# The residual transposed before it is normalized, the router put between output products, and the second block's loads asked for at other places

## What is computed

```python
def rms_norm(x, w):
    y = xf * lax.rsqrt(jnp.mean(xf * xf, axis=-1, keepdims=True) + NORM_EPS)
    return (y * w.astype(jnp.float32)).astype(x.dtype)

# layer 0 (block A)
h = h + ssd_memory_mixer(h, mem, a_norm_w[i], ...)     # ends in [y, m] @ out_w
h = h + hierarchical_moe(h, ffn_norm_w[0], ...)
# layer 1 (block B)
k_sh, v_sh = shared_kv(h, kv_norm_w, w_kv, positions)  # rms_norm(h) @ w_kv
h = h + swa_memory_mixer(h, k_sh, v_sh, mem, ...)      # rms_norm(h) @ in_w gives q and q_mem
h = h + hierarchical_moe(h, ffn_norm_w[1], ...)
return rms_norm(h, final_norm_w)

def hierarchical_moe(h, norm_w, rg_w, rg_b, re_w, re_b, w_gate, w_up, w_down):
    xt = rms_norm(h, norm_w).reshape(-1, d)
    group_p = jax.nn.softmax((xt @ rg_w) + rg_b)        # 4 groups, the best one
    exp_logits = (xt @ re_w) + re_b                     # 8 experts in a group, the best two
    ...
    for e in range(32):
        out = out + gates[:, e:e + 1] * ((silu(xt @ w_gate[e]) * (xt @ w_up[e])) @ w_down[e])
```

## Time and profile before

| | |
|---|---|
| three runs | 1459.13, 1455.79, 1454.13 us; median 1455.79 |
| the profiled execution, its own time | 1459.73 us |
| its span, first to last instruction | 1457.9 us (1.8 us less than its time) |
| PE, DVE, ACT, POOL busy | 1230.5, 278.1, 199.1, 33.4 us |
| read from HBM | 456.66 MB |
| mean granted TensorE clock | 0.919 of 2.4 GHz |

### The profile page before, as it was taken

One profiled execution on the slowest core, in us unless ns is written; L12 is line 12 of the kernel. 1 busy time (PEld: TensorE's weight loads), 2 busy tenths in 40 slices (PEclk: granted clock), 3 DMA queues, 4 the chain that ended last, 5 costly groups with the idle time before them and its releaser, 6 DMA issues. The chain is left out here.

```text
span 1457.9 us, 15099 instructions
## 1 busy us (share of the span) xinstructions
PE 1230.5 (84%) x6038; PEld 623.7 (43%) x6038; DVE 278.1 (19%) x691; ACT 199.1 (14%) x491; POOL 33.4 (2%) x42
## 2 busy tenths in 40 slices
PE   6999999889999997687643998979999999666664
PEld 6875874444443453232211466454444444222211
DVE  3542451221010100000002156022011101000001
ACT  3133231100000000000001145110000000000001
POOL 0001210000000000000000011000000000000000
PEclk9999999889999999889886999969999999778877
DMA  9534207459999999999998222538999999999994
GB/s 368 208 116 140 92 26 320 173 229 417 419 416 416 413 419 369 419 410 418 419 397 302 107 83 86 203 116 336 418 416 416 418 417 417 418 415 421 414 418 163
DMA packets 93897, 458.76 MB, mean 315 GB/s; under 512 B 7040, under 2 KB 7040, under 8 KB 60672
## 3 DMA queue, kind: packets, MB, share of 16 engines
q1 hardware_dynamic: 93824, 457.74, 78.3%
HBM read 456.66 MB, written 1.05 MB: 314 GB/s over the span
## 5 line engine op out<-in xcount | busy, mean ns | idle before, releaser
L1358 PE MATMUL bank<-own,e_xg 128*64 128x512 f32 (+1 forms) x1312 | 279.6, 664 | 41.4 <-DMA own<-in_w_up 18.4
L1358 PE MATMUL bank<-late,e_xg 128*64 128x512 f32 (+1 forms) x736 | 181.9, 676 | 35.6 <-DMA own<-in_w_up 19.5
L1367 PE MATMUL bank<-own,e_turned 128*32 128x512 f32 (+1 forms) x656 | 146.8, 707 | 48.2 <-DMA own<-in_w_down 34.3
L1358 PEld LDWEIGHTS bank<-own,e_xg 128*64 128x64 f32 (+1 forms) x1312 | 80.8, 134 | 199.1 <-issue 199.0
L1250 DVE TENSOR_TENSOR e_hid<-e_silu,bank 128x512 f32<-128x512 f32 x24 | 16.5, 688 | 515.0 <-ACT e_silu L1301 515.0
L1367 PE MATMUL bank<-late,e_turned 128*64 128x512 f32 (+1 forms) x368 | 91.0, 699 | 21.9 <-DMA own<-in_w_down 9.1
L1358 PEld LDWEIGHTS bank<-late,e_xg 128*64 128x64 f32 (+1 forms) x736 | 51.2, 135 | 133.8 <-issue 133.8
L1333 PE MATMUL bank<-e_pick,xs 128*128 128x128 f32 x768 | 101.1, 287 | 3.9 <-DVE e_pick L1197 2.3
L1333 PEld LDWEIGHTS bank<-e_pick,xs 128*128 128x128 f32 x768 | 94.1, 200 | 22.7 <-issue 18.0
L1367 PEld LDWEIGHTS bank<-own,e_turned 128*32 128x32 f32 (+1 forms) x656 | 41.2, 139 | 126.2 <-issue 119.5
L1301 ACT ACTIVATE e_silu<-bank 128x512 f32<-128x512 f32 x24 | 14.3, 597 | 554.9 <-PE bank L1358 554.9
(11 more groups left out here) (297 smaller groups left out, 1022.6 us busy)
## 6 DMA issues: line engine op xcount, KB each, us to landing
own<-in_w_up SPq DMA_DIRECT2D x83, 1024.0 KB, 14.3
own<-in_w_down SPq DMA_DIRECT2D x82, 1024.0 KB, 15.0
own<-in_w_gate SPq DMA_DIRECT2D x81, 1024.0 KB, 15.2
late<-in_w_gate SPq DMA_DIRECT2D x47, 1024.0 KB, 16.7
late<-in_w_down SPq DMA_DIRECT2D x46, 1024.0 KB, 14.2
late<-in_w_up SPq DMA_DIRECT2D x45, 1024.0 KB, 14.4
own<-in_a_in_w SPq DMA_DIRECT2D x18, 1024.0 KB, 12.1
own<-in_mem_w_kv SPq DMA_DIRECT2D x8, 1024.0 KB, 11.2
```

What stands on the lines that cost most here:

```text
L1358: ins = pe.matmul(bank[q * T:(q + 1) * T, :], self.xg[:, at:at + T], cut(tile(q), k=4)[:, k, :], start=(half == 0 and k == 0), stop=(half ...
L1367: ins = pe.matmul(self.b_down[out][q * T:(q + 1) * T, :], self.turned[:, at:at + T], cut(tile(q), j=2)[:, j, 512 * out:512 * out + 512], s ...
```

## The change

- **Residual transposed raw.** `x2T` (both routers) and `xT` (block B) transpose `h` itself. The factor is computed alongside: the logits are multiplied by it (`scalar_tensor_tensor` with the bias), in block B the evictions of q, k, v, and the softmax scale of the memory scores. The columns of the weights are laid out for that (`by_block`, `blocks`, `(k p)` in place of `(p k)`). The scaled `xs`, which the experts' gather reads, is now written by ACT.
- **Order of the end of a mixer.** The last tile's products are split by quarter, the transposes of t = 0 come after `("out", 1)`, its logits between `("out", 2)` and `("out", 3)`. Evictions of `x2T` alternate between ACT and DVE. `choose` works on all 32 experts at once and takes the group's mask afterwards; two chains are interleaved; the counts are separate products after the places.
- **Gather.** The second half goes to a bank of its own (`b_turn`).
- **Loads of block B.** Four (two tiles) are issued in `moe(c, 0)` ahead of the wait for the last down product; the other ten in `mixer_b`. q comes first, then kv; the first banks used are 4 to 7.
- **Final norm.** Its weight is loaded at the start of `moe(c, 1)` into an unused tensor.

```diff
-    NORMED = [("x2T", 0), ("x2T", 1), ("router", 0)]
-    UNITS = NORMED + [("x2T", 2), ("x2T", 3), ("router", 1), ("places", 0)]
+    UNITS = [("out", 0), ("out", 1), ("x2T", 0), ("x2T", 1), ("out", 2), ("router", 0), ("out", 3), ("x2T", 2), ("x2T", 3),
+             ("router", 1), ("places", 0)]
@@ out_rows
+    if i == 0:
+        for m in range(n, last):
+            some(0, m, (0, 1))
+    if i == 2:
+        for m in range(n + 1, last):
+            some(1, m, (0, 1)).then_inc(s["out_tile"], 1)
+    some(t, last, (i % 2,)).then_inc(c.units_done, 1)
+    if i == 1:
+        some(1, n, (0, 1)).then_inc(s["out_tile"], 1)
@@ Router.act
+        if kind == "x2T" and i % 2 == 0:
+            t = i // 2
             U.wait_done(act, key)
+            act.activation(self.x2T(i), cut(U.bank(key), k=4), ACT.Copy).then_inc(s["x2T_act"], 1)
+            act.wait_ge(s["h_new"], 2 * t + 2)
+            h, xs = cut(c.h, t=NT)[:, t, :], cut(c.xs[:, :], t=NT)[:, t, :]
+            act.activation(xs, h, ACT.Square, accum_out=self.ss[t]).then_inc(s["n2_act"], 1)
+            act.wait_ge(s["n2_dve"], 2 * t + 1)
+            act.activation(self.r[t], self.ss[t], ACT.Sqrt).then_inc(s["n2_act"], 1)
+            act.wait_ge(s["n2_dve"], 2 * t + 2)
+            act.activation(xs.rearrange("q (k p) -> q p k", k=KD), h.rearrange("q (p k) -> q p k", k=KD), ACT.Copy,
+                           scale=self.r[t]).then_inc(s["n2_act"], 1)
@@ Router.pe
-            pe.wait_ge(s["n2_dve"], 3 * t + 3)
+            pe.wait_ge(s["h_new"], i + 1)
+            transposes(c, pe, out, [cut(c.h, t=NT)[:, t, (4 * half + k) * P:(4 * half + k + 1) * P] for k in range(4)])
@@ Router.dve
+            dve.wait_ge(s["n2_dve"], 2 * i + 2)
+            dve.scalar_tensor_tensor(out=cut(self.lg, t=NT)[:, i, :], in0=U.bank(key)[:, 0:NG + NE], scalar=self.r[i],
+                                     in1=c.f(f"route_b{self.layer}"), op0=ALU.mult, op1=ALU.add).then_inc(s["rt_dve"], 1)
@@ Experts.block, sync
+                if layer == 1:
+                    final_w = c.ins["final_norm_w"].rearrange("(o n) -> o n", o=1)
+                    sp.dma_start(c.memT1[:, 0:D], final_w.broadcast_to([P, D])).then_inc(c.final_w, 16)
...
+                if layer == 0:
+                    for n in range(B0, B0 + FIRST_TILES):
+                        for half in range(2):
+                            sp.wait_ge(*self.released(before(("mixer", n, half))))
+                            c.load_mixer_half(sp, n, half)
                 sp.wait_ge(*self.released(jobs[-1]))
                 self.over_rounds(sp, body)
-                if layer == 0:
-                    for n in range(B0, B0 + TILES_B):
-                        for half in range(2):
-                            job = ("mixer", n, half)
-                            if before(job)[0] != "mixer":
-                                sp.wait_ge(*self.released(before(job)))
-                                c.load_mixer_half(sp, n, half)
@@ Experts.block, tensor
                 gather(0, s["gathered"])
-                pe.wait_ge(s["xg_ready"], 1)
-                gather(1, s["gathered"])
+                gather(1, s["gathered"], self.b_turn)
@@ mixer_b
-        order = [("xT", i) for i in range(4)] + [("kv", 0), ("kv", 1), ("q", 0), ("q", 1), ("kT", 0), ("kT", 1), ("qm", 0), ("qT", 0), ("qT", 1)]
+        order = [("xT", i) for i in range(4)] + [("q", 0), ("q", 1), ("kv", 0), ("kv", 1), ("qT", 0), ("qT", 1), ("qm", 0), ("kT", 0), ("kT", 1)]
@@ mixer_b, scalar
+                    if i == 3:
+                        act.wait_ge(s["h_whole"], 4)
+                        for t in range(NT):
+                            act.activation(cut(c.xs[:, :], t=NT)[:, t, :], cut(c.h, t=NT)[:, t, :], ACT.Square,
+                                           accum_out=ss[:, t:t + 1]).then_inc(s["x_act"], 1)
@@ mixer_b, tensor
-                    if i == 0:
-                        pe.wait_ge(s["x_dve"], 6)
-                    norm_T_units(c, pe, out, i)
+                    pe.wait_ge(s["h_whole"], 2 if i < 2 else 4)
+                    transposes(c, pe, out, [cut(c.h, t=NT)[:, t, (2 * i + kk) * P:(2 * i + kk + 1) * P] for kk in range(2) for t in range(NT)])
@@ mixer_b, vector
-            for t in range(NT):
-                finish_h(c, dve, t, s["h_whole"])
-            for t in range(NT):
-                norm.dve(dve, t)
+            for q in (0, 2, 1, 3):
+                finish_h(c, dve, q, s["h_whole"])
```

More of the change, by code:

```diff
@@ L140 @@
 FIRST_JOBS = SLOTS
+FIRST_TILES = 2
+KEPT = [JOB_AT["mixer", B0 + n, half][0] for n in range(FIRST_TILES) for half in range(2)]
+OVER_SLOTS = [slot for slot in range(SLOTS) if slot not in KEPT]
 def before(job):
@@ L285, with __init__ @@
 class Units:
-    def __init__(self, core, order, freed, holds=None):
+    def __init__(self, core, order, freed, holds=None, first=0):
         self.core, self.freed = core, freed
@@ L297, in __init__ @@
         held = [key for keys in holds.values() for key in keys]
-        free, user, self.of, self.before = list(range(NBANK)), {}, {}, {}
+        free, user, self.of, self.before = [*range(first, NBANK), *range(first)], {}, {}, {}
         for key in order:
@@ L358, in memory_rows, with out_rows, some @@
         ins.then_inc(s["out_tile"], 1)
[L361 to L366, removed]
-            for half in range(2):
[L368 to L374, removed]
+def out_rows(c, pe, U, s, src, n, tiles, i):
+    t, last = i // 2, n + tiles - 1
+    def some(t, m, halves):
+        c.wait_tile(pe, m)
+        for half in halves:
+            for j in range(4):
+                ins = pe.matmul(U.bank(("out", 2 * t + half))[:, :], src(t, 4 * (m - n) + j), c.rows_at(m, j)[:, 512 * half:512 * half + 512],
+                                start=False, stop=(m == last and j == 3))
+        return ins
+    if i == 0:
[7 more added lines that the diff above has]
+        some(1, n, (0, 1)).then_inc(s["out_tile"], 1)
 def project(c, pe, out, lhsT, rhs, n=KD):
@@ L445, in freed @@
+        w = [NT * (NG + NE), NT * NG, NT * NG] + [NT * NE] * 5 + [NT] * 3 + [NT * NG] * 7
+        (self.lg, self.ge, self.g1, self.eq, self.o1, self.o2, self.l2, self.mask, self.gm, self.gi, self.gs, self.m1, self.m2, self.i_,
+         self.dd, self.ed, self.w1, self.w2) = (work[:, sum(w[:i]):sum(w[:i + 1])] for i in range(len(w)))
     @staticmethod
     def freed(s, kind, i):
-        return {"x2T": (s["x2T_ev"], i + 1), "router": (s["rt_dve"], i + 1), "places": (s["rt_dve"], Router.PLACES)}[kind]
@@ L565, in choose @@
[L565 to L570 removed]
+        step(dve.tensor_scalar(self.w2, self.ed, 1.0, None, ALU.add))
@@ L1506, in mixer_b @@
                 order += [("av", n - 3)]
-        order += [("out", i) for i in range(4)] + Router.UNITS
+        order += Router.UNITS
         holds = {("outm", h): [("out", i) for i in range(4)] for h in range(4)}
@@ L1516, in freed @@
                     "out": (s["h_new"], i + 1)}[kind]
-        U = Units(c, order, freed, holds)
+        U = Units(c, order, freed, holds, first=4)
         R = Router(c, U, s, 1, xnT, sb("work", 512))
-        norm = Norm(c, c.h, 0, s["x_act"], s["x_dve"])
+        ss, rr = c.norm_ss[:, 0:NT], c.norm_r[:, 0:NT]
         def tile_used(n):
-            last = [("kv", 1), ("q", 1), ("q", 3), ("qm", 3)]
+            last = [("q", 1), ("kv", 1), ("q", 3), ("qm", 3)]
             if n - B0 < 4:
@@ L1565, in _ @@
         def _(act):
-            norm.warm(act)
-            for t in range(NT):
-                act.wait_ge(s["h_whole"], 2 * t + 2)
-                norm.act(act, t)
+            act.activation(c.norm_r[:, 6:7], c.norm_ss[:, 4:5], ACT.Sqrt)
             for key in order:
```

293 lines of the change are left out of this document (158 added, 135 removed).

## The result

The changed kernel takes 1408.48 us, the median of 4 runs (1407.45 to 1409.6), against 1456.73 us for the kernel before on the same chip (4 runs, 1454.13 to 1459.13). The ratio is 0.9669, 95% interval 0.965 to 0.9689. The profiled execution took 1409.6 us, its span 1407.8, at a mean granted clock of 0.935.

A forecast was written before the change was run, and what follows sets the result against it. Expert stages were taken as bound by their weight streams, block B by PE, leaving the joints between stages to gain. Joint terms summed to 35.7 us off the 1455.8 us median, giving 1420 us, range 1411 to 1431.

The forecast's parts named there:

- the one on the streams: Both expert stages: each ends at its start plus a fixed stream of weights, so an earlier start is gained in full.
- the rival of a slower one: Expert weight streams: should their rate fall to 390 GB/s, they would take 51 us more, 1471 us; chance 0.03.
- Block's end: Layer 0's experts to block B: with only four loads issued before it, DVE starts earlier, 14.2 us gained.
- Raw transposes: Block B's start: transposing the raw residual shortens first sum to first product from 11.82 to 5.95 us, 5.9 us gained.
- Block A with choose and gather: Block A to layer 0's experts: 4.9 us from the router among the products, 0.8 from choose, 0.8 from the gather.
- Block B with choose and gather: Block B to layer 1's experts: 5.8 us from the router among the products, 0.8 from choose, 0.8 from the gather.
- Final weight: Program's end: loading the final norm's weight earlier removes DVE's wait of 1.73 us, 1.7 us gained.
- choose: Expert choice after the logits: fewer, partly interleaved steps save 0.8 us in each layer, bounds 0 and 1.5.
- The early loads: Rival at layer 0's experts' end: block B's four loads delay the last expert weights, at worst 10 us, 1430 us; chance 0.08.
- TensorE's clock: Rival at block B's start and the gathers: the clock stays up, gaining more there, 1415 us; chance 0.08.
- The gather: Start of each layer's experts: the second half no longer waits for DVE, 0.8 us gained in each layer.
- The Block's end is not SP's: Rival at layer 0's experts' end: another release holds it, so joint 1 gains only 5.9 us, 1434 us; chance 0.07.

The follow-up runs named there:

- own_at_192_in_new: Changed kernel with 48 unused columns ahead of the weight slots, which then begin 192 bytes past a multiple of 256 again: 1420.93 us, ratio to before 0.9743.
- loads_back: Changed kernel with all loads of block B issued where they were before the change: 1423.61 us, ratio to before 0.977.
- loads_only_in_old: Kernel before with only the loads of block B moved as in the change: 1443.91 us, ratio to before 0.9898.

## Why the prediction was wrong

**The step that failed** is the one on the streams: "In both expert stages ... the end of such a stage is its start plus a fixed stream of weights", and, under the rival of a slower one, "I see no cause in the change". The rate was taken as fixed. It depends on where in SBUF the slots begin, and the change moved them by 64 B through two small fields. That gave 12.5 us (`own_at_192_in_new`) of the 48 us, about the 11.5 by which the forecast missed. The rival had the lever right, the stream's rate, but only with the other sign, and I looked for its cause in the order of loads and not in the layout.

The sentence fails in a second way that cost nothing here: the earlier trace rows are averages over 450 us, and the stage of layer 0 isn't held by its stream up to SP's hold at 546 us. A gain in the rate is lost there (4.3 us against 7.4 in layer 1), while an earlier start is still gained in full.

**The joints were right.** With the slots displaced as before, the new kernel takes 1420.93, 37.5 us less than its kernel before; the sum was 35.7. Term by term: Block's end forecast 14.2, in the trace 14.5, by the two runs 15.1 and 13.3. Raw transposes forecast 5.9, in the trace 6.6: the transposes took 2.73 us instead of 3.68. Block A with choose and gather forecast 6.5, in the trace 6.5. Block B with choose and gather forecast 7.4, in the trace 8.8: it takes 176.48 us from its first product to the first released slot (771.92 to 948.40), 185.3 before (804.00 to 989.3). In it the router's part is 5.8, as forecast (8.73 us less from the last sum to the logits, 2.96 more from the first product to that sum), and most of the surplus is the gather's, 2.0 where 0.8 was forecast. Final weight forecast 1.7, in the trace 1.7.

**choose** was forecast at 0.8 and gave 1.04. The scaled copy of h on ACT lasted 2.03 us and lay beside it, as assumed.

**The early loads** did not delay the expert weights: that wait fell from 6.52 to 4.63 us in the trace, and with the loads put back it is 4.62 (755.35, `loads_back`). The rival falls.

**TensorE's clock** did fall at the joint. By window around block B's first product, in the kernel after:

```profile
766.00:768.00 2.00, 0.00 (x0) 0.00 (x0) 1.28 (x3) 1.30 (x2) 0.00 (x0) 1.00 0.11 22
...
770.00:772.00 2.00, 0.87 (x5) 0.50 (x3) 1.89 (x4) 2.00 (x6) 0.00 (x0) 0.50 1.05 405
...
776.00:778.00 2.00, 2.00 (x5) 0.89 (x4) 0.00 (x0) 0.00 (x0) 0.00 (x0) 0.86 1.05 410
```

PE stood still or worked in pieces from 765.5 to 771.9; the granted clock, still 1.00 (2.4 GHz) at 766, was 0.50 (1.2 GHz) at 770 and was back in the window from 776, so the first product ran at half speed for some 4 to 5 us, as it did before. The rival of a clock that stays up falls here. Elsewhere it moved times by a microsecond or two, as the next point shows.

**The gather** was forecast at 0.8 us in each layer, for the wait that goes. Right in mechanism, wrong in both sizes, which add up to little. From the places to the first expert product it took 9.69 us in layer 0 (293.08 to 302.77) and takes 9.65 now (286.58 to 296.23): nothing gained, because the second half, which ran at 2.05 us behind its wait, now runs mostly at the lower clock with the first (granted 0.50 from 290 to 294, 0.68 to 296; 6.38 us for both). In layer 1 both halves had been slow, 3.78 us the second one; there it was 11.76 us (973.88 to 985.64) and is 9.72 (934.99 to 944.71): 2.0 gained. What layer 0 missed was made up by its logits, 5.5 us earlier (288.22 to 282.76) where 4.9 were forecast. That block A's total was hit to 0.1 us is therefore luck.

**The Block's end is not SP's** falls by the 0.44 us in `loads_back` and by `loads_only_in_old`.

## What to carry to other kernels

A kernel that is held by its loads has a rate that depends on the address of their destination: before pricing an edit, look where its new tensors push the buffers, and start large load buffers at a multiple of 256 B. It costs one unused tensor, and here it was worth 12.5 us of 1421 and 13.7 of 1458. When two versions differ in rate with the same loads, move only the address in both before believing any other cause. An average over a stage hides a stretch where another engine sets the pace: before pricing a faster stream, look for windows in which the DMA engines idle. And an engine that is held while it issues loads (here SP, until 0.44 us before DVE went on) holds a barrier that waits for all engines: loads that aren't urgent belong behind the barrier. Here that was worth 13 to 15 us.

## What the hardware showed unexpectedly

- Loads of 1 MB into slots that begin 64, 128 or 192 B past a multiple of 256 B moved at 417 GB/s, at a multiple of 256 or 512 B at 424, with the DMA engines' busy share at 1.02 in both. The share doesn't show the loss.
- Displacing 11 of the 17 slots cost 4.1 us, displacing the other 6 (with what lies behind them) cost 2.7, which is within the noise, displacing all cost 12.5.
- A pause that is shortened isn't gained in full where PE runs at the lower clock behind it: the new router order won 6.7 us ahead of the gathers and lost 2.2 in them.
- In layer 0 the DMA engines stood at a share of 0.33 and 111 GB/s from 540 to 550 us, because SP waited for a slot behind 64 products of PE. The faster rate gained nothing ahead of this and 4.3 us behind it.
